# x and w_ada transposed by the host, modulation by DVE row sums, x scaled by features, first passes ordered by kind

## The reference

```python
c_act = jax.nn.silu(c)                                  # [1, 1024]
mod = jnp.einsum('bd,de->be', c_act, w_ada[l]) + b_ada[l]   # w_ada [1024, 6144]
shift1, scale1, gate1, shift2, scale2, gate2 = jnp.split(mod, 6, axis=-1)
hmix = modulate(rmsnorm(x, g_norm1[l]), shift1, scale1)  # h*(1+scale)+shift
proj = jnp.einsum('bsd,de->bse', hmix, w_in[l])
...
x = x + gate1[:, None, :] * jnp.einsum('bsd,de->bse', merged, w_out[l])
```

## Time and profile before

| | before |
|---|---|
| time, median of 3 runs (lowest to highest) | 1888.11 us (1887.7 to 1888.24) |
| span of the profiled execution | 1888.1 us |
| PE busy | 1859.0 us, 98% |
| PEld busy | 1454.0 us, 77% |
| DVE busy | 859.6 us, 46% |
| ACT busy | 686.3 us, 36% |
| POOL busy | 552.0 us, 29% |
| moved by DMA | 192.46 MB, mean 102 GB/s |

### The profile page before, as it was taken

How to read it: one execution, slowest core, us unless ns; L and a number is a source line. 1 busy time by engine, 2 the same in 40 slices (tenths; PEclk the granted TensorE clock), 3 DMA queues, 4 the chain that set the end, 5 groups by cost and what they waited for, 6 DMA issues and landing times.

```text
span 1888.1 us, 21529 instructions
## 1 busy us (share of the span) xinstructions
PE 1859.0 (98%) x8653; PEld 1454.0 (77%) x8653; DVE 859.6 (46%) x1348; ACT 686.3 (36%) x1023; POOL 552.0 (29%) x437
## 2 busy tenths in 40 slices
PE   6999999999999999999999999999999999999998
PEld 6777778877777777877888888877776788888886
DVE  6467542646261303324333333548777654423433
ACT  5555542223232323433222222435546532212223
POOL 3543344445355544431000000044556211100100
PEclk9999999999999999999999999999999999999999
DMA  9412223544343122322423322432221222222321
GB/s 300 149 50 68 68 68 123 164 147 155 120 150 110 62 74 85 130 94 87 131 79 100 112 89 70 109 95 79 87 92 58 74 90 93 90 89 91 104 87 54
DMA packets 182332, 192.46 MB, mean 102 GB/s; under 512 B 10155, under 2 KB 166065, under 8 KB 181977
## 3 DMA queue, kind: packets, MB, share of 16 engines
q1 hardware_dynamic: 179704, 180.84, 29.8%
q0 software_dynamic: 1104, 5.24, 1.0%
q10 hardware_dynamic: 1424, 5.00, 0.7%
HBM read 188.95 MB, written 4.72 MB: 103 GB/s over the span
## 4 chain that ended last, share of the span: by engine, by line
PE 93%; DVE 4%; ACT 2%; issue 1%; DMA 0%; ACTq 0%; SPq 0%; DVEq 0%
PE bank L1492 25%; PE bank L1497 24%; PE bank L1494 24%; PE bank L1517 2%; PE bank L1515 2%; PE bank L1513 2%; PE bank L1591 2%; PE bank L1525 2%; PE bank L1541 1%; PE bank L1561 1%; PE bank L1577 1%; DVE left L1859 1%; DVE ADA L1817 1%; PE bank L1471 1%; PE bank L1477 1%
## 5 line engine op out<-in xcount | busy, mean ns | idle before, releaser
L1492 PE MATMUL bank<-hH,wh 128*128 128x512 f32 x1264 | 520.4, 412 | 3.3 <-ACT hH L2221 3.0
L1497 PE MATMUL bank<-hL,wh 128*128 128x512 f32 x1264 | 501.4, 397 | 0.1
L1494 PE MATMUL bank<-hH,wl 128*128 128x512 f32 x1264 | 501.3, 397 | 0.0
L2606 POOL TENSOR_TENSOR wl<-stg,wh 128x512 fp32r<-128x512 f32 x150 | 200.0, 1333 | 792.3 <-ACT wh L2238 792.0
L2238 ACT ACTIVATE wh<-stg 128x1024 fp32r<-128x1024 f32 (+2 forms) x292 | 298.2, 1023 | 271.5 <-PE bank L1497 191.3
L1492 PEld LDWEIGHTS bank<-hH,wh 128*128 128x128 f32 x1264 | 238.4, 189 | 76.0 <-issue 23.3
L1497 PEld LDWEIGHTS bank<-hL,wh 128*128 128x128 f32 x1264 | 238.3, 189 | 58.1 <-DVE hL L1973 0.5
L1494 PEld LDWEIGHTS bank<-hH,wl 128*128 128x128 f32 x1264 | 239.1, 189 | 53.4 <-issue 2.6
L1799 DVE TENSOR_TENSOR wl<-stg,wh 128x1024 fp32r<-128x1024 f32 (+2 forms) x142 | 168.3, 1188 | 240.0 <-ACT wh L2238 239.5
L2607 POOL TENSOR_TENSOR wl<-stg,wh 128x512 fp32r<-128x512 f32 x150 | 203.8, 1359 | 0.0
L1492 PE MATMUL bank<-h2H,wh 128*128 128x512 f32 x352 | 140.6, 399 | 0.0
(11 more groups left out here) (326 smaller groups left out, 2599.8 us busy)
## 6 DMA issues: line engine op xcount, KB each, us to landing
stg<-in_w_in SPq DMA_DIRECT2D x54, 1024.0 KB, 5.1
stg<-in_w_ffn_in SPq DMA_DIRECT2D x22, 1024.0 KB, 5.1
stg<-in_w_ada SPq DMA_DIRECT2D x16, 1024.0 KB, 5.3
stg<-in_w_ffn_gate SPq DMA_DIRECT2D x11, 1024.0 KB, 5.2
stg<-in_w_ffn_up SPq DMA_DIRECT2D x11, 1024.0 KB, 5.1
stg<-in_w_ffn_down SPq DMA_DIRECT2D x10, 1024.0 KB, 5.0
stg<-in_w_ada SPq DMA_DIRECT2D x16, 512.0 KB, 6.4
stg<-in_w_proj_ret SPq DMA_DIRECT2D x8, 1024.0 KB, 5.0
```

Source lines behind the costliest of these rows:

```text
L1492: T.matmul(ps, wh, xh, start=j["first"] and k == 0, stop=False)
L1494: T.matmul(ps, wl, xh, start=False, stop=False)
L1497: t = T.matmul(ps, wh, xl, start=False, stop=j["stop"] and last)
L2606: G.tensor_tensor(lo[:, 0:h, :], src[:, 0:h, :], hi[:, 0:h, :], ALU.subtract)
```

## The change

x, `w_ada` and the small vectors arrive in another layout: `x_t` with features on the partitions, `w_ada_t` with one output of the modulation on each partition and its 1024 inputs along the row, `cols` already in columns, and the 768 columns of `w_in` for each first pass in one piece. silu(c) is taken as one row of 1024 and spread over all partitions by two matmuls with a row of ones (`cb`), copied into the SBUF tile `CB`. `ada` becomes two operations on DVE for each 1 MB piece, each a product of 1024 elements of `stg` with `CB` and its row sum; `adasum` is gone. x is squared tile by tile on ACT, added on DVE, and averaged over features by four fp32 matmuls (`n1_sum`); ACT makes 1/rms from it (`factor`) and DVE scales each tile (`xr`). `xt` and `x2t` are gone. The 18 matmuls of a first pass come as six high by high, six low weights, six `hL`. The step `norm1` of tile k stands ahead of pass k, and pass k is no longer two places behind. The tile `rlog` gives way to `SQ`, `ADA` goes, and the eight `tmp` tiles become one tensor `tmps`.

```diff
     def ada(self, a, b):
-        for k in range(KT):
-            if k:
+        for half in range(2):
+            if half:
                 yield
-            self.emit("ada", a, k)
...
-            take("Z", ("mod", a), 0)
-            emit("adasum", a)
-            give(("mod", a))
...
-        p.job(p.block("w_ada", a * 256), 0, ada_job(a), last=True, ada=a)
+        p.job(p.block(None, 0, src=[("w_ada_t", half, 2 * a + half) for half in range(2)]), 0, ada_job(a), last=True, ada=a)
...
     def setup():
-        take("Z", "rows")
+        for half in range(2):
+            take("C", ("cb", half))
         emit("setup")
-        give("rows")
-        emit("x_square")
-        p.bank["ada_acc"] = (4, 0, 0)
-        p.busy.add(4)
+        emit("c_silu")
+        emit("x_square", 0)
+        emit("x_square", 1)
+        emit("cb")
+        for half in range(2):
+            give(("cb", half))
+        emit("x_square", 2)
+        emit("x_square", 3)
+        take("Z", "n1")
+        emit("n1_sum")
+        factor("n1")
     do(setup)
...
     def norm1(k):
         emit("mod1", k)
-        give(("mod1", k))
+        emit("xr", k)
+        if k == KT - 1:
+            give("n1")
         p.split("h1", k, "pool")
         emit("n1", k)
...
         def fn(n):
-            if k == 0:
-                emit("x_norm")
-                turn_x1(range(4))
-            for i, _ in enumerate(p.jobs[n]["steps"]):
-                if i == 2 and k:
-                    norm1(k - 1)
-            if k == 1:
-                turn_x1(range(4, 8))
-            take("Z", ("mod1", k), 0)
-            emit("adasum", k)
+            for _ in p.jobs[n]["steps"]:
+                pass
...
     def first_job(k):
         def fn(n):
             p.parts(n)
-            if k:
-                first_gemm(n - 2)
+            norm1(k)
+            first_gemm(n)
             if k < KT - 1:
                 return
-            p.busy.remove(4)
-            norm1(k)
             emit("masks")
-            first_gemm(n)
...
-        b = p.block(None, 0, src=[("w_ada", 0, k * P, P), ("w_ada", P, D + k * P, P)])
+        b = p.block(None, 0, src=[("w_ada_t", 0, k), ("w_ada_t", 1, KT + k)])
...
         def fn(n):
-            take("Z", ("x2t", f))
-            emit("x2t", f)
...
             def setup():
-                nc.sync.dma_start(TMP[0][0:NROWS, 0:P], a["rows"]).then_inc(s["d_rows"], 16)
-                nc.sync.dma_start(ident[:, :], a["k_mats"][:, 0, :]).then_inc(s["d_ident"], 16)
+                nc.sync.dma_start(crow, a["c"].rearrange("o (k t) -> o k t", k=2)).then_inc(s["d_c"], 16)
+                for i in (0, 1):
+                    nc.sync.dma_start(X[:, 2 * i:2 * i + 2, :], a["x_t"][:, 2 * i:2 * i + 2, :]).then_inc(s[f"d_x{i}"], 16)
             def row_load(k):
                 if k >= 3:
                     sp.wait_ge("w_lo_pool", k - 2)
-                for e in range(3):
-                    nc.sync.dma_start(ROW[k % 3][:, 256 * e:256 * e + 256], a["w_in"][0, k * P:(k + 1) * P, D * e:D * e + 256]).then_inc(
-                        s[f"d_row{k % 3}"], 16)
+                nc.sync.dma_start(ROW[k % 3][:, :], a["w_row"][k]).then_inc(s[f"d_row{k % 3}"], 16)
                 if k == 2:
-                    nc.sync.dma_start(matf[:, :, :], a["k_mats"][:, 1:5, :]).then_inc(s["d_matf"], 16)
+                    nc.sync.dma_start(ident[:, :], a["k_mats"][:, 0, :]).then_inc(s["d_ident"], 16)
+                    nc.sync.dma_start(matf[:, 1:4, :], a["k_mats"][:, 2:5, :]).then_inc(s["d_matf"], 16)
...
+                if blk["src"][0][0] == "w_ada_t":
+                    for w, half, tile in blk["src"]:
+                        nc.sync.dma_start(STG[b % 3][:, D * half:D * half + D], a[w][tile]).then_inc(s[f"d_stg{b % 3}"], 16)
...
-            def adasum(n):
-                key = ("mod1" if n < 8 else "mod", n)
+            def cb():
                 pe.wait_ge("v_set", 1)
-                zb = free(pe, key)
-                pe.wait_ge("ada", 8 * (n + 1))
-                acc = ada_sum(n)
-                T.matmul(zb[:, 0:1], acc[:, 0:P], one, start=True, stop=True)
-                T.matmul(zb[:, 1:2], acc[:, P:2 * P], one, start=True, stop=True).then_inc(s["pe_ada"], 1)
-            def xt(k):
-                gb = free(pe, ("xt", k))
-                pe.wait_ge("v_x", 5)
-                for i in range(4):
-                    t = T.matmul(gb[:, i * P:(i + 1) * P], X[:, i, k * P:(k + 1) * P], TMP[6][:, i * P:(i + 1) * P], start=True, stop=True)
-                t.then_inc(fill(("xt", k)), 1)
+                pe.wait_ge("cact", 1)
+                for half in range(2):
+                    T.matmul(free(pe, ("cb", half))[:, :], ones, crow[:, half, :], start=True, stop=True).then_inc(fill(("cb", half)), 1)
+            def n1_sum():
+                zb = free(pe, "n1")
+                pe.wait_ge("v_set", 3)
+                pe.wait_ge("v_xa", 2)
+                T.matmul(zb[:, :], MEAN[D], TMP[4], start=True, stop=False)
+                T.matmul(zb[:, :], MEAN[D], TMP[5], start=False, stop=False)
+                pe.wait_ge("a_x", 4)
+                T.matmul(zb[:, :], MEAN[D], TMP[6], start=False, stop=False)
+                pe.wait_ge("a_x", 5)
+                T.matmul(zb[:, :], MEAN[D], TMP[7], start=False, stop=True).then_inc(fill("n1"), 1)
...
-                for e in range(6):
-                    ps = (free(pe, ("first", e)) if k == 0 else BANK[bank["first", e][0]])[:, :]
-                    wh, wl = hi[:, 0, e * P:(e + 1) * P], lo[:, 0, e * P:(e + 1) * P]
-                    T.matmul(ps, wh, xh, start=k == 0, stop=False)
-                    if e == 0:
-                        pe.wait_ge("w_lo_" + j["lo"], j["low"])
-                    T.matmul(ps, wl, xh, start=False, stop=False)
-                    if e == 0:
-                        low_done(pe, "h1", k)
-                    t = T.matmul(ps, wh, xl, start=False, stop=k == KT - 1)
+                banks = [(free(pe, ("first", e)) if k == 0 else BANK[bank["first", e][0]])[:, :] for e in range(6)]
+                cols = [slice(e * P, (e + 1) * P) for e in range(6)]
+                for ps, c in zip(banks, cols):
+                    T.matmul(ps, hi[:, 0, c], xh, start=k == 0, stop=False)
+                pe.wait_ge("w_lo_" + j["lo"], j["low"])
+                for ps, c in zip(banks, cols):
+                    T.matmul(ps, lo[:, 0, c], xh, start=False, stop=False)
+                low_done(pe, "h1", k)
+                for e, (ps, c) in enumerate(zip(banks, cols)):
+                    t = T.matmul(ps, hi[:, 0, c], xl, start=False, stop=k == KT - 1)
                     if k == KT - 1 or e == 5:
                         t.then_inc(s["gemm"], 1)
...
-                pe.wait_ge("d_xa", 16)
-                zb = free(pe, ("x2t", f))
-                for i in range(4):
-                    t = T.transpose(zb[:, i * P:(i + 1) * P], X2[:, i, f * P:(f + 1) * P], ident[:, :])
-                t.then_inc(fill(("x2t", f)), 1)
...
+            def x_square(i):
+                if i in (1, 2):
+                    ve.wait_ge("a_x", i + 1)
+                    if i == 2:
+                        ve.wait_ge("v_xa", 1)
+                    V.tensor_tensor(tmps[:, 4:6, :], tmps[:, 4:6, :], tmps[:, 2 * i - 2:2 * i, :], ALU.add).then_inc(s["v_xa"], 1)
...
-            def ada(n, k):
+            def ada(n, half):
                 b = next(j["b"] for j in jobs if j["ada"] == n)
-                view = STG[b % 3][:, :].rearrange("p (k c) -> p k c", k=KT)
-                acc, last = ada_sum(n), ada_sum(n)
-                if n < 8:
-                    acc = BANK[bank["ada_acc"][0]][:, 256 * (n % 2):256 * (n % 2) + 256]
-                    if k < KT - 1:
-                        last = acc
-                if k == 0:
+                w, tile = STG[b % 3][:, D * half:D * half + D], p.blocks[b]["src"][half][2]
+                if half == 0:
                     ve.wait_ge(f"d_stg{b % 3}", p.blocks[b]["landed"])
-                    ve.wait_ge("cact", 1)
-                    if n >= 2:
-                        ve.wait_ge("pe_ada", n - 1 if n < 8 else n)
-                    V.tensor_scalar(last, view[:, 0, :], cact[:, 0:1], None, ALU.mult).then_inc(s["ada"], 1)
-                else:
-                    ve.wait_ge("ada", 8 * n + k)
-                    V.scalar_tensor_tensor(last, view[:, k, :], cact[:, k:k + 1], acc, ALU.mult, ALU.add).then_inc(s["ada"], 1)
...
+                    for e in range(2):
+                        emptied(ve, ("cb", e))
+                V.tensor_tensor_reduce(w, w, CB[:, :], 1.0, C("b_ada", tile), ALU.mult, ALU.add, mod[:, tile:tile + 1]).then_inc(s["ada"], 1)
...
             def mod1(k):
-                zb = BANK[bank["mod1", k][0]]
-                ve.wait_ge("pe_ada", k + 1)
-                ve.wait_ge("v_set", 5)
-                V.tensor_tensor(mod[:, k:k + 1], zb[:, 0:1], col[:, 8 + k:9 + k], ALU.add).then_inc(s["v_a1"], 1)
```

(46 more changed lines are left out.)

116 lines of the change are left out of this document (44 added, 72 removed).

## The result

The changed kernel takes 1883.72 us (median of 10 runs, 1882.75 to 1884.85), the kernel before 1888.28 beside it: ratio 0.9973, 95% interval 0.9965 to 0.9981. It is faster by some 4.6 us, where 10.5 were forecast. The profiled execution has a span of 1882.5 us against 1888.1, a difference of 5.6. Time and span are not the same quantity: in every run that lists both, the time is 1.8 us longer (1.76 to 1.93; here 1884.31 and 1882.5).

A forecast was written before the change was run, and what follows sets the result against it. PE, busy 98%, bounds the kernel, with DVE and POOL turns setting the first passes after the change. Start and passes -0.2, handover +0.9, `adasum` -7.7, `x2t` -3.5 sum to -10.5 from 1888.1: 1877.6 us, range 1871 to 1885.

The forecast's parts named there:

- `xr` of tile 0 starts: DVE's first use of the norm factor, scaling the first tile of x; forecast at 20.8 us.
- seven periods: First passes, from the scaling of tile 0 to that of tile 7: 7 x 5.03 us.
- from there to the ordinary jobs: After the scaling of tile 7: `n1` and `hH` 1.5 us, then the pass 4.2; ordinary jobs at 62.3.
- handover: Where ordinary jobs begin: 0.5 us wait behind ACT's four copies, exponentials later too; 0.9 us taken, between 0 and 1.7.
- `adasum`, its wait, `x2t`: PE work removed after the first passes: 7.0 us for `adasum`, 0.7 for its wait, 3.5 for `x2t`.
- The start: Before the first pass: x landed at about 8.3, sum of squares 6.4 us, first pass at 23.2, 2.8 us earlier.
- The period of a pass: First passes: DVE's sums and POOL take turns at SBUF, making 5.0 us a pass, more than PE's 4.2.
- The last stretch: From tile 7's scaling to the ordinary jobs: `n1` and `hH` 1.5 us, pass 4.2, ending at 62.3.
- Later: Retention and `x2t` stages: 7.7 us gained from `adasum` and its wait, 3.5 from `x2t`; retention sums cost nothing.
- A: First passes: row-output sums don't exclude POOL, or POOL uses DVE's gaps; PE sets the pass, 1874.2 us; chance 0.19.
- B: First passes: sums with two SBUF inputs go at half rate, 7.2 us a pass, about 1894 us; chance 0.08.
- C: Start slips: x lands late or silu, `cb` and squares queue; some 5 us late would give 1883; chance 0.10.

The follow-up runs named there:

- e7: Changed kernel with dummy fp32 matmuls on TensorE, 14 ahead of the sum of squares and 8 ahead of the first pass; 1881.54 us, ratio 0.9961.
- e5: Changed kernel with `mod1` still on VectorE but as a tensor_scalar with one tensor input, g as scalar operand; 1880.46 us, ratio 0.9953.
- e3: Changed kernel with VectorE's sums of tile k+1 ordered ahead of the scaling of tile k; 1883.21 us, ratio 0.9971.
- e4: Changed kernel with the first passes bank by bank again, in place of ordered by kind; 1884.79 us, ratio 0.9977.
- e6: Changed kernel with `mod1` issued twice for each tile, the second into a spare column; 1883.60 us, ratio 0.9972.
- e1: Changed kernel with `mod1` worked out on ScalarE instead of VectorE; 1880.08 us, ratio 0.9952.
- e2: Changed kernel with `mod1` on ScalarE and the first 8 tiles' sums reading silu(c) from PSUM, their modulation values not right; 1875.86 us, ratio 0.9933.

## Why the prediction was wrong

The span, by the prediction's own steps:

| step | forecast | changed kernel | off by |
|---|---|---|---|
| `xr` of tile 0 starts | 20.8 | 21.32 | +0.5 |
| seven periods | 7 x 5.03 = 35.2 | 38.69 | +3.5 |
| from there to the ordinary jobs | 6.3 | 8.22 | +1.9 |
| handover | +0.9 | 0.0 | -0.9 |
| `adasum`, its wait, `x2t` | -11.2 | -11.35 | -0.15 |

The sum is +4.9, which is 1882.5 - 1877.6. On the medians, which the forecast is measured by, 1883.72 - 1877.6 is 6.1: the other 1.2 us are the step from span to time, 1.8, less the 0.6 by which this traced execution was longer than the median. The forecast took the span of 1888.1 for the median, which it is not (its execution took about 1889.9).

**The start** was right to 0.5 us, partly by luck, for two errors went against each other. The second quarter of x was there at 9.9 us, where all of x was to have landed by 8.3, so the sum of squares began at 14.33 where about 12.9 follows from the forecast; and it took 5.5 us where 6.4 were taken, since only half of it was slow. By e7 the slow half costs 1.8 us (3.7 in place of 5.5).

**The period of a pass is the step that failed**, where it has "`mod1` (0.2)" in DVE's 3.5 us and "Period: 1.8 + 1.24 + 2 x 1.0 = 5.0". The mechanism was right: DVE with two SBUF inputs and POOL exclude each other, and the sums with a row output do so too. But `mod1` was costed by its length, though it has two SBUF tensor inputs as well. The argument that gave the sums their turns applies to it, whatever its size. 0.2 us is what the old `mod1` took (0.21, L1838), with one of its tensors in PSUM. The new one waits 0.95 to 1.5 us in each tile but the first; e5 takes the second tensor input away and gets 34.9 us for the seven periods.

**The last stretch** missed the clock. The prediction saw the fall of the clock after a gap for the first pass, by the earlier trace rows, and hid it under the period. It forecast gaps between the later passes and did not ask what the clock does in them. The seventh pass was 1.55 us longer, and the last pass could only start behind it, at 64.02. In e5 and e7, where the seventh pass is not slow, the stretch is 6.7. Each of the five kernels that keep the third turn (the changed one, e3, e4, e6, e7) has one later pass at the low clock; none of the ten others has, and no gap between their passes is over 1.6 us. Which of several gaps is followed by the low clock is not settled: 2.36 us was (58.19), 2.35 and 2.32 were not (36.20, 47.18), in e7 it was another one, and in e4 gaps of 0.82 and 1.22 us stood ahead of it.

**The handover** was forecast at +0.9 and is nothing here (7.91 against 7.92 us). It costs 0.5 us in e1 and e5, where PE waits for `wl` on POOL, and not for the copies on ACT that the forecast had, and at most 0.15 in the other kernels on this base (by the steps of ACT behind the start of the jobs), those with earlier jobs included. Why it is these two isn't shown.

**Later**: both terms in full, 7.97 for `adasum` and its wait (forecast 7.7) and 3.40 for `x2t` (3.5). The sums in the retention stages cost nothing that these numbers show.

**Rivals.** A was false, and e2 made it true by taking the shared reads away. B was false: a sum over 1024 elements takes 1.27 us alone. There the Trainium skill (Vector Engine (DVE) Microarchitecture Reference, Points that are easy to get wrong) has half the throughput for the shape `S2S2D2_STT` with two non-bf16 SBUF sources. The trace doesn't agree. The sum is recorded as another operation (CUSTOM_DVE_ANT_0) and goes at full rate; and a scalar-tensor-tensor of the changed kernel with two SBUF tensors, without a row sum, takes as long as one with a tensor in PSUM (both of 512 elements):

```profile
L1938 DVE SCALAR_TENSOR_TENSOR hL<-tmps,mod,hH x8: 747/748/752, 846.7 to 855.6; 128x512 fp32r<-128x512 f32 x8
L1963 DVE SCALAR_TENSOR_TENSOR XR<-bank,mod,XR x16: 743/750/752, 998.4 to 1221.9; 128x512 f32<-128x512 f32 x16
```

C cost 0.5 us in `xr` of tile 0; x itself was later than that, as said of the start.

## What to carry to other kernels

Where VectorE and GpSimd share a stage, list every VectorE instruction with two SBUF tensor inputs, the 128x1 ones first: each that arrives while GpSimd works costs up to one GpSimd instruction, and a scalar operand or a PSUM input avoids it. A stage that goes by turns has little slack: a load 0.21 us late cost nothing, one 0.45 us late went with a tile that took 1.26 longer. And before two traces are compared by what is left behind a stage, see whether a stretch that the edit doesn't touch differs between them: here it was up to 1.4 us. When a forecast puts idle time between stretches of TensorE, cost the next stretch at both clocks.

## What was not expected of the hardware

- A 128x1 VectorE operation with two SBUF tensors took 1.66 us beside a GpSimd subtraction, 0.16 alone, and 0.21 beside it both with one tensor and a scalar operand and with one of its two tensors in PSUM.
- Of two such operations in a row the second never waited, in seven tiles: 1.67 and 0.15 us.
- The same 24 matmuls behind the same gap of 3.04 us took 7.0 us in one kernel and 8.4 in another, the low clock (0.50) lasting for more or fewer of them.
- Sums over 512 columns with one input in PSUM and subtractions on GpSimd run side by side at 0.74 and 1.85 us, as each does alone.
